# Token rows of an expert gathered as half rows onto 128 partitions in place of whole rows onto 64

## The reference

```
x = x + mixer(rms_norm(x, g_mix));  h = rms_norm(x, g_ffn)
group  = argmax over 4 of (h @ w_group + b_group)
expert = the two best of the 8 experts of that group, by h @ w_er[group] + b_er[group]
gate   = softmax(the two values) * softmax(group logits)[group]
y[token] = sum over its two experts of gate * ((silu(h @ w_gate[e]) * (h @ w_up[e])) @ w_down[e])
x = x + y
```

## Time and profile before

| what | value |
|---|---|
| median of the runs | 1629.51 us |
| profiled execution, span from first to last instruction | 1627.8 us |
| PE busy | 1416.6 us (87%) |
| DVE, ACT, POOL busy | 528.0, 243.8, 191.6 us |
| bytes moved by DMA | 479.22 MB |
| share of the chain of waits: PE, DMA | 19%, 18% |

### The profile page before, as it was taken

How to read it: one execution, slowest core, us unless ns; L and a number is a source line. 1 busy time by engine, 2 the same in 40 slices (tenths; PEclk the granted TensorE clock), 3 DMA queues, 4 the chain that set the end, 5 groups by cost and what they waited for, 6 DMA issues and landing times. The chain is left out here.

```text
span 1627.8 us, 19016 instructions
## 1 busy us (share of the span) xinstructions
PE 1416.6 (87%) x7093; PEld 662.4 (41%) x7093; DVE 528.0 (32%) x1240; ACT 243.8 (15%) x522; POOL 191.6 (12%) x362
## 2 busy tenths in 40 slices
PE   6999999999888878887889978999988788778886
PEld 3544574553333323332333546455333233323232
DVE  6999983351101110111150179134111111101114
ACT  3202111210000000000020157121000000000002
POOL 5200000011111111111000000001111111111100
PEclk9999999999999998999999989999999899989998
DMA  8325345479999999999994100547999999999995
GB/s 246 113 71 84 48 149 226 164 296 367 398 411 406 406 406 415 404 409 404 421 357 152 52 1 13 232 181 275 357 402 416 403 412 400 413 400 410 406 420 230
DMA packets 74021, 479.22 MB, mean 294 GB/s; under 512 B 17204, under 2 KB 24116, under 8 KB 49392
## 3 DMA queue, kind: packets, MB, share of 16 engines
q1 hardware_dynamic: 61392, 454.36, 71.5%
q0 software_dynamic: 11152, 19.27, 3.6%
q10 hardware_dynamic: 1424, 4.89, 0.8%
HBM read 468.01 MB, written 26.74 MB: 304 GB/s over the span
## 5 line engine op out<-in xcount | busy, mean ns | idle before, releaser
L686 PE MATMUL psum<-ring,work 128*64 128x512 f32 x992 | 488.4, 650 | 118.1 <-DMA ring<-in_moe_w_up 118.1
L687 PE MATMUL psum<-ring,work 128*64 128x512 f32 x992 | 488.6, 650 | 0.0
L686 PEld LDWEIGHTS psum<-ring,work 128*64 128x64 f32 x992 | 143.6, 150 | 436.7 <-issue 347.6
L699 PE MATMUL psum<-ring,work 128*64 128x512 f32 x992 | 226.4, 598 | 28.2 <-DVE work L872 28.2
L869 DVE TENSOR_TENSOR work<-work,psum 64x512 f32<-64x512 f32 x64 | 44.1, 690 | 598.7 <-ACT work L826 598.6
L826 ACT ACTIVATE work<-psum 64x512 f32<-64x512 f32 x64 | 37.8, 590 | 830.3 <-PE psum L687 830.3
L687 PEld LDWEIGHTS psum<-ring,work 128*64 128x64 f32 x992 | 143.5, 150 | 2.5 <-issue 1.0
L699 PEld LDWEIGHTS psum<-ring,work 128*64 128x64 f32 x992 | 66.9, 136 | 142.9 <-issue 126.2
L875 DVE COPY work<-psum 128x512 f32<-128x512 f32 x60 | 41.5, 692 | 231.1 <-PE psum L699 231.1
L1779 PE MATMUL psum<-ring,hT 128*128 128x512 f32 x256 | 112.0, 593 | 0.0
L1065 POOL COPY ints<-ints 64x1 uint32 (+1 forms) x64 | 12.2, 190 | 524.7 <-PE psum L678 495.4
(11 more groups left out here) (380 smaller groups left out, 1409.9 us busy)
## 6 DMA issues: line engine op xcount, KB each, us to landing
ring<-in_moe_w_gate SPq DMA_DIRECT2D x62, 2048.0 KB, 17.7
ring<-in_moe_w_up SPq DMA_DIRECT2D x62, 2048.0 KB, 23.0
ring<-in_moe_w_down SPq DMA_DIRECT2D x62, 2048.0 KB, 23.3
ring<-in_hyb_w_in SPq DMA_DIRECT2D x5, 2048.0 KB, 9.0
work<-y_dram SPq DMA_DIRECT2D x8, 1024.0 KB, 8.7
ring<-in_swa_w_qkv SPq DMA_DIRECT2D x3, 2048.0 KB, 17.1
x_sb<-in_x SPq DMA_DIRECT2D x8, 512.0 KB, 6.7
y_dram<-x_sb SPq DMA_DIRECT2D x1, 4096.0 KB, 18.6
```

The costliest lines, as they stand in the source:

```text
L686: nc.tensor.matmul(bank[2 + b][0:BLK, :], XT[b][:, c, :], g[:, c, :], start=c == 0, stop=c == KC - 1)
L687: i = nc.tensor.matmul(bank[2 + b][BLK:P, :], XT[b][:, c, :], u[:, c, :], start=c == 0, stop=c == KC - 1)
L699: i = nc.tensor.matmul(bank[6 + b][BLK * hf:BLK * (hf + 1), :], HTE[b][:, c, :], d[:, c, hf * HALF:(hf + 1) * HALF], start=c == 0, stop=c ...
```

## The change

Norms 1 and 3 write their rows in another column order: feature 8q + 4g + c goes to column 512g + 4q + c. So the first half of a stored row holds the features whose number modulo 8 is 0 to 3, the second half the others. `h_dram` is declared as 1024 half rows of 512. The lists of the gather hold half-row numbers, 2 * token on partitions 0 to 63 and 2 * token + 1 on 64 to 127, so L445 and L459 are made twice, once for each half of the partitions. The gather brings 128 half rows to `XG[b]`, now 128 partitions x 512. Four transposes of 128x128 replace eight of 64x128, and the gate and up matmuls take their columns from the new layout of `XT`. The norm's one DVE operation over 1024 columns becomes two over 512, with a wait between them.

```diff
-    put("tok", np.arange(NT)[None, :] * P + p[:, None] - NOROW)
+    put("tok", 2 * (np.arange(NT)[None, :] * P + p[:, None]) - 2 * NOROW)
...
-        h_dram = dram("h_dram", [S, D])
+        h_half = dram("h_dram", [2 * S, HALF])
+        h_dram = h_half.rearrange("(s h) d -> s (h d)", h=2)
...
-            V(nc.vector.scalar_tensor_tensor(hN[:, t, :], xv[:, t, :], ss[3], GN[:, :], ALU.mult, ALU.mult), n_h)
+            if n % 2 == 0:
+                V(nc.vector.scalar_tensor_tensor(hN[:, t, :], xv[:, t, :], ss[3], GN[:, :], ALU.mult, ALU.mult), n_h)
+                return
+
+            xt, gn = (a.rearrange("p (q g c) -> p q g c", g=2, c=4) for a in (xv[:, t, :], GN[:, :]))
+            o = hN[:, t, :].rearrange("p (g q c) -> p g q c", g=2, c=4)
+            V(nc.vector.scalar_tensor_tensor(o[:, 0], xt[:, :, 0], ss[3], gn[:, :, 0], ALU.mult, ALU.mult))
+            V.sync()
+            V(nc.vector.scalar_tensor_tensor(o[:, 1], xt[:, :, 1], ss[3], gn[:, :, 1], ALU.mult, ALU.mult), n_h)
...
-                    i = nc.tensor.transpose(bank[norm_bank(n, t) + hf][:, c4 * P:(c4 + 1) * P],
-                                            hN[:, t, 4 * hf + c4::KC], ident)
+                    cols = hN[:, t, HALF * hf + c4:HALF * (hf + 1):4] if n % 2 else hN[:, t, 4 * hf + c4::KC]
+                    i = nc.tensor.transpose(bank[norm_bank(n, t) + hf][:, c4 * P:(c4 + 1) * P], cols, ident)
...
-        XG = [WK[0:BLK, 8192 + 1024 * b:9216 + 1024 * b] for b in range(2)]
-        XT = [cut(WK, 10240 + 512 * b, 512).rearrange("p (c n) -> p c n", c=KC) for b in range(2)]
+        XG = [cut(WK, 8192 + HALF * b, HALF) for b in range(2)]
+        XT = [cut(WK, 10240 + 512 * b, 512).rearrange("p (c n) -> p c n", c=4) for b in range(2)]
...
-                i = nc.tensor.matmul(bank[2][0:BLK, 0:NE], pl[:, a, :], bl[:, a, :], start=a == 0, stop=a == 7)
+                for hf in range(2):
+                    i = nc.tensor.matmul(bank[2][BLK * hf:BLK * (hf + 1), 0:NE], pl[:, a, :], bl[:, a, :], start=a == 0,
+                                         stop=a == 7)
...
-                nc.tensor.matmul(bank[4][0:BLK, 256:256 + NBLK - NE], pl[:, a, :], bl[:, a, :], start=a == 0, stop=a == 7)
+                for hf in range(2):
+                    nc.tensor.matmul(bank[4][BLK * hf:BLK * (hf + 1), 256:256 + NBLK - NE], pl[:, a, :], bl[:, a, :],
+                                     start=a == 0, stop=a == 7)
...
-            V(tv.tensor_scalar(SLL[:, 0:NE], bank[2][0:BLK, 0:NE], float(NOROW), None, ALU.add), g_sl)
+            V(tv.tensor_scalar(SLL[:, 0:NE], bank[2][:, 0:NE], cst("half"), 2.0 * NOROW, ALU.add, ALU.add), g_sl)
...
-            for c in range(KC):
-                i = nc.tensor.transpose(bank[b][:, c * BLK:(c + 1) * BLK], XG[b][:, c::KC], ident[0:BLK, 0:BLK])
+            for c in range(4):
+                i = nc.tensor.transpose(bank[b][:, c * P:(c + 1) * P], XG[b][:, c::4], ident)
...
-                nc.tensor.matmul(bank[2 + b][0:BLK, :], XT[b][:, c, :], g[:, c, :], start=c == 0, stop=c == KC - 1)
-                i = nc.tensor.matmul(bank[2 + b][BLK:P, :], XT[b][:, c, :], u[:, c, :], start=c == 0, stop=c == KC - 1)
+                x = XT[b][:, c % 4, BLK * (c // 4):BLK * (c // 4 + 1)]
+                nc.tensor.matmul(bank[2 + b][0:BLK, :], x, g[:, c, :], start=c == 0, stop=c == KC - 1)
+                i = nc.tensor.matmul(bank[2 + b][BLK:P, :], x, u[:, c, :], start=c == 0, stop=c == KC - 1)
...
-                pool.indirect_dma_start(XG[b], None, h_dram, bass.IndirectOffsetOnAxis(STG[b], 0), bounds_check=S - 1,
+                pool.indirect_dma_start(XG[b], None, h_half, bass.IndirectOffsetOnAxis(STG[b], 0), bounds_check=2 * S - 1,
                                         oob_is_err=False).then_inc(done, 16)
```

More of the change, by code:

```diff
@@ L387, in encoder @@
         OVI = INTS[:, 20:20 + MAXOV + 2]
-        SLL = INTS[0:BLK, 64:64 + NBLK]
-        STG = [INTS[0:BLK, 64 + NBLK + b:65 + NBLK + b] for b in range(2)]
+        SLL = INTS[:, 64:64 + NBLK]
+        STG = [INTS[:, 64 + NBLK + b:65 + NBLK + b] for b in range(2)]
         SCL = rt("At")[:, 0:NBLK].bitcast(U32)
@@ L626, in dve_router @@
             dve.wait_ge(g_Om.s, 2 * l + 1)
-            V(tv.tensor_scalar(SLL[:, NE:NBLK], bank[4][0:BLK, 256:256 + no], float(NOROW), None, ALU.add))
+            V(tv.tensor_scalar(SLL[:, NE:NBLK], bank[4][:, 256:256 + no], cst("half"), 2.0 * NOROW, ALU.add, ALU.add))
             V(tv.tensor_scalar(SCL[:, NE:NBLK], bank[5][:, 256:256 + no], cst("half"), 2.0 * NOROW, ALU.add, ALU.add))
@@ L822, in act_xe @@
         def act_xe(b, done):
-            nc.scalar.copy(XT[b], bank[b][:, :].rearrange("p (c n) -> p c n", c=KC)).then_inc(done, 1)
+            nc.scalar.copy(XT[b], bank[b][:, :].rearrange("p (c n) -> p c n", c=4)).then_inc(done, 1)
         def act_silu(b, done):
```

## The result

| | before | after |
|---|---|---|
| median of 4 runs (lowest to highest) | 1629.88 us (1624.0 to 1631.56) | 1588.86 us (1584.55 to 1592.88) |
| span of the profiled execution | 1627.8 us | 1582.7 us |

The ratio is 0.9756, with a 95% interval of 0.9734 to 0.9779: the change makes the kernel 41 us faster, where 23.5 were forecast.

A forecast was written before the change was run, and what follows sets the result against it. DMA transport was taken to bound both mixture-of-experts stages, with PE counting only at each layer's head. Gathers 22.5 us plus head 1 us made 23.5 us, giving 1606 us; own range 1592 to 1614, with chance 0.60.

The forecast's parts named there:

- The bound: In both mixture-of-experts stages DMA transport sets the pace, except PE for some five experts at each layer's head.
- The main term: Gathers in the saturated stretches: 128 half rows on 128 partitions save 0.5 us each, 45 x 0.5 = 22.5 us.
- between the two gains: The 0.5 us per gather was chosen between 0.75 us (whole excess gone) and 0.37 us (loss halved with the bytes).
- The head, 1 us: First experts of each layer: transposes less lists and norm gain 1.1 us per layer, 2.2 for both; 1 us counted.
- four transposes: Per expert on PE: 0.52 us instead of 1.02, worth 2.5 us per layer at the head, nothing in the saturated stretch.
- The doubled lists: L445 and L459 go from 8 to 16 matmuls: +0.6 us each, 1.2 us per layer; ends nothing and +1.1 each.
- The norm's pair: One 1285 ns DVE operation becomes two of 692 ns: +0.15 us per layer with the wait; ends 0 and +1.3.
- POOL: Issue of the gather: from 973 ns to the 128-partition scatter's 1016, 43 ns more, costing nothing.
- A: Rival: loss comes from reading scattered rows or crowded places, so only the head's 1 us is left: 1628 us; chance 0.20.
- B: Rival: loss goes by descriptor on the gather's read side, 128 lose twice what 64 do: 1663 us; chance 0.13.
- C: Rival: PE at its lower clock frees slots late and half the gain, 12 us, is lost: 1617 us; chance 0.07.
- The late end: After the change DMA is still late; the period per expert falls from 16.3 us to 15.8.

The follow-up runs named there:

- e6: The two kernels, before and changed, with gathers that bring no rows from the fifth expert of each layer on (56 gathers): 1571.18 and 1571.6 us.
- e1: Kernel before with each whole-row gather split into two gathers of 64 half rows, both still onto partitions 0 to 63: 1633.5 us, ratio 1.0014.
- e5: Kernel before with whole 4 KB rows gathered onto 128 partitions, half of the tokens on each half (half computed from old rows): 1609.31 us, ratio 0.9870.
- e8: Kernel before with odd experts' rows gathered onto partitions 64 to 127, even ones' onto 0 to 63: 1631.21 us, ratio 1.0011.
- e2: Kernel before with token i of an expert on partition i instead of the order of `place`: 1634.69 us, ratio 1.0017.
- e3: Changed kernel with token i on partitions i and 64 + i instead of the order of `place`: 1597.79 us, ratio 0.9801.
- e4: Changed kernel with each expert's four transposes issued twice: 1589.57 us, ratio 0.9774.
- e6a: Changed kernel with empty gather lists from the fifth expert of each layer on, same 128 descriptors, no row moved: 1571.6 us, ratio 0.9673.
- e6b: Kernel before with empty gather lists from the fifth expert of each layer on, same 64 descriptors, no row moved: 1571.18 us, ratio 0.9666.
- e9: Changed kernel with token i on partition 8 * (i mod 8) + i div 8 (and 64 more): 1615.19 us, ratio 0.9921.
- e7: Kernel before with whole rows gathered onto 128 partitions, gather lists empty from the fifth expert of each layer on: 1574.55 us, ratio 0.9656.

## Why the prediction was right in kind and short in size

**The bound**: right. The DMA engines set the pace in both stages before and after, and the time follows GB/s.

**The main term, 45 gathers x 0.5 us: the step that failed.** The mechanism held, the size didn't, in both of its factors. The excess was measured by the windows as 0.75 us. The long windows say the same: the earlier trace rows against 427 GB/s are 380 x 18/427 + 405 x 20/427 = 35 us lost, over 46 gathers 0.76 each. I knew the 0.75 and took 0.5, "between the two gains", because "a gather, unlike the scatter, still writes where the weights write". That reason was worth nothing: the windows behind gathers went to 422, not to the middle. The measured time therefore lies even below the range that I had written for this mechanism, whose lower end was meant for the whole 0.75 (1592 in the text; its own sum, 45 x 0.75 + 2, gives 1594).

The count was too small as well, though by less. "The gathers of the first experts fall where DMA has gaps and count nothing" holds for the first seven of a layer and not for those behind them. Here are the windows from the seventh gather of layer 0 to the eighth and from there to the ninth, before and then after:

```profile
389.77:402.15 12.38, 12.38 (x66) 5.21 (x64) 2.38 (x4) 1.18 (x2) 2.35 (x5) 1.00 0.94 351
402.15:414.70 12.55, 11.90 (x62) 4.73 (x60) 1.93 (x4) 1.18 (x2) 2.35 (x5) 1.00 1.01 401
```

```profile
388.42:400.79 12.37, 12.23 (x62) 4.86 (x60) 2.46 (x4) 1.18 (x2) 2.43 (x4) 1.00 0.91 355
400.79:413.19 12.40, 11.54 (x58) 4.33 (x54) 1.80 (x3) 1.18 (x2) 2.41 (x4) 1.00 1.00 422
```

Up to the eighth gather the DMA engines have gaps in both kernels, and a loss before them is made up in them. From the eighth on the share is full and before's rate is low, though PE still sets the pace: that transport is missed later. So three gathers of layer 0 and two of layer 1 come to the 45, and 50 x 0.76 = 38 us is an estimate of the main term. (e6 can't say how many count: it removes the rows of 56, and its 0.73 is the whole gain divided by 56.) Of the 17.5 us that the forecast missed, some 12 come from the size (45 x 0.26), 4 from the count (5 x 0.76), and the last 2 are the head and what two single executions can't tell apart.

The Trainium skill, SBUF — State Buffer, section "Door 1: The DMA port swizzle", says that partitions 0 to 63 reach half of the ports and 64 to 127 the other half. e1, e5 and e8 agree that a gather spread over both halves costs less than one on either half, though no run shows a port, and whether the weights wait at ports or at DMA engines isn't told apart. The gain estimated from it, 0.6 us per gather, is below the measured 0.76, and its working doesn't fit e5: by the port map e5 puts the first 32 tokens on 4 ports, 32 KB each, as the kernel before does, only two of the ports in each half, and the hole is closed all the same. By its port map a list in order spreads the first 32 tokens over twice the ports that `place` does, yet e2 is no faster than the kernel before and e3 is no faster than the change, so the map alone doesn't order these runs.

**The head, 1 us.** Too small to tell in the median. From the first gather of a layer to the tenth the time fell from 88.1 to 86.7 us in layer 0, and with the doubled transposes of e4 it is 88.3; at the last scatter only 0.5 us of that 1.6 is left between e4 and the change (1.2 of 1.7 in layer 1). So part of what PE gains at the head ends in the wait for DMA, as the forecast had it when it counted 1 us of 2.2. By terms: four transposes take 0.47 us on the chain (0.52 forecast). The doubled lists cost 1.13 against 1.09 us for L455, and L471 takes 1.04 where before's L459 has 1.03 on the chain: nothing, where I had 0.6 each; the halves run beside each other, the lower of my two ends. The norm's pair takes 0.75 + 0.04 + 0.75 = 1.54 us against 1.285, +0.25 and not +0.15. Layer 0's head gained 1.0 us. e6a equals e6b within 6 us, so all of this together is worth less than can be measured.

**POOL**: the gather's issue rose from 973 to 1043 ns, not 1016, and costs nothing, as said.

**The rivals.** A (no gain): the hole closed. That the order of the places could matter was a right question, as e3 and e9 show (9 and 26 us), but it isn't what the gain is made of. B (loss by descriptor): e1 has 128 list entries in two gathers and stays at 364 GB/s. The number of packets in q0, 11152 before and after, doesn't bear on it (see the last section). The Trainium skill, DMA: Bandwidth & Descriptors, section "Why small descriptors are slow", which I had set against the change, would have made the gather's packets some 2% dearer, by the estimate in the prediction; no run here can tell so little, and the windows behind gathers rose from 362 to 422 GB/s. C (PE's clock): the granted clock rose from 0.92 to 0.95, with PE busy 299 of 360 us (0.83) where it was busy 311 of 380 (0.82); nothing was given back.

**The late end.** The period fell to 15.4 us, taken as in the prediction (438.26 to 762.66 for the same 21 gathers); the rates alone, 16.3 x 409/427, give 15.6. PE is busy 299 of 360 us, so DMA is still what is late; with the rows of 56 gathers gone the time is 1571 us, so some 17 us are left to win at this place, and they include the time of the rows' own bytes.

## What to carry to other kernels

Beside a saturated stream of loads look at the rate in short windows laid behind each kind of small transfer: a few hundred KB lost each time is invisible in the busy share, which stays full, and is worth 2.5% here. Let a transfer's on-chip side span both halves of the partitions, even at the price of shorter runs, and then compare orders of its list, since they moved the time by up to 26 us. When such an excess is measured and an equal transfer beside it shows none, count all of it, from the instance on at which the DMA share is full (which can be before the rate looks full), and don't halve it for want of a reason.

## What I had not expected of the hardware

- The number of packets in q0 says nothing of how rows travel. It is 11152 for gathers of 64 rows of 4 KB and for gathers of 128 half rows of 2 KB, and it is 11152 too in e6a and e6b, where 56 gathers bring no row and the queue's bytes fall from 19.27 to 11.88 MB. e5, whose lists have 128 entries of 4 KB with at least half of them out of range, has 64 more for each of its 64 gathers, and e7, where 56 of the lists are wholly out of range, has exactly as many as e5. So the count follows the length of the list times the length of a row, whether the entries are in range or not; the expectation of e7, which says that empty entries travel singly, read too much into it. q0 of e6a, e5 and e7:

```profile
q0 software_dynamic: 11152, 11.88, 2.3%
```

```profile
q0 software_dynamic: 15248, 19.29, 3.5%
```

```profile
q0 software_dynamic: 15248, 11.93, 2.5%
```

- Gathers whose list is empty from end to end leave no hole in the stream (e6a and e6b read 425 and 426 GB/s over 440:800).
- The DMA share passes 1.0 with one queue alone, and not only with two in flight as I wrote above: in the window 90:93 of the earlier trace rows q1 by itself holds 104.1%.
- Sixteen list matmuls of 32 columns take 1.13 us where eight took 1.09, when the added eight write the other half of the partitions.
